# Four tiles of products with the raw x ahead of the first norm, with the norm's factor put in where they are evicted

## The reference

```python
def rms_norm(x, g):
    xf = x.astype(jnp.float32)
    y = xf * lax.rsqrt(jnp.mean(xf * xf, axis=-1, keepdims=True) + EPS)
    return (y * g.astype(jnp.float32)).astype(x.dtype)
...
    h = rms_norm(x, norm_g)
    q, k, v, z = jnp.split(h @ w_in, 4, axis=-1)
    q = rms_norm(q.reshape(b, s, DA_HEADS, 2, DA_HEAD), q_norm_g) * (DA_HEAD ** -0.5)
    k = rms_norm(k.reshape(b, s, DA_HEADS, 2, DA_HEAD), k_norm_g)
    v = v.reshape(b, s, DA_HEADS, DA_VDIM)
```

## Time and profile before

| | |
|---|---|
| median of 3 runs | 1915.85 us |
| profiled execution, its own time | 1915.09 us |
| its span | 1913.3 us |
| TensorE (PE) busy | 1873.1 us, 98% |
| VectorE (DVE) busy | 988.9 us, 52% |
| ScalarE (ACT) busy | 815.8 us, 43% |
| GpSimd (POOL) busy | 124.2 us, 6% |
| DMA | 201.95 MB, mean 106 GB/s |
| mean granted clock of TensorE | 0.994 |

### The profile page before, as it was taken

The page is one execution under the profiler, slowest core; times in us unless marked ns, Lnnn a source line. Parts: engine busy times, 40 slices in busy tenths (PEclk is TensorE's granted clock), DMA queues, the critical chain, the costliest instruction groups (busy, mean ns, idle before and its releaser), DMA issues.

```text
span 1913.3 us, 22366 instructions
## 1 busy us (share of the span) xinstructions
PE 1873.1 (98%) x8923; PEld 1452.5 (76%) x8923; DVE 988.9 (52%) x1764; ACT 815.8 (43%) x1325; POOL 124.2 (6%) x148
## 2 busy tenths in 40 slices
PE   7999999999999999999999999999999999999997
PEld 4666666666788788888886777677888878888886
DVE  4566667666544643333347566854434673333322
ACT  5466556656643342222324555434432342222221
POOL 0111111110001000000010011000000100000000
PEclk9999999999999999999999999999999999999999
DMA  5334334332233132222223222221023322322221
GB/s 213 147 144 150 137 143 155 143 144 99 78 118 123 69 110 99 94 96 92 99 95 117 93 72 88 84 94 34 34 96 113 121 89 99 99 93 97 97 93 62
DMA packets 56526, 201.95 MB, mean 106 GB/s; under 512 B 6478, under 2 KB 6934, under 8 KB 55784
## 3 DMA queue, kind: packets, MB, share of 16 engines
q1 hardware_dynamic: 44616, 158.32, 23.6%
q0 software_dynamic: 11808, 42.21, 6.1%
HBM read 195.23 MB, written 5.28 MB: 105 GB/s over the span
## 4 chain that ended last, share of the span: by engine, by line
PE 76%; DVE 12%; ACT 9%; issue 2%; DMA 1%; POOL 0%; DVEq 0%; SPq 0%; ACTq 0%
PE ps L1111 22%; PE ps L1114 22%; PE ps L1112 22%; ACT wH L1820 2%; DVE wL L1404 2%; PE ps L1209 2%; PE ps L1173 1%; DVE a L1533 1%; PE ps L1197 1%; DVE a L1699 1%; ACT a L1931 1%; PE ps L1185 1%; PE ps L1245 1%; PE ps L1144 1%; DVE b L1464 1%
## 5 line engine op out<-in xcount | busy, mean ns | idle before, releaser
L1111 PE MATMUL ps<-hH,wH 128*128 128x512 f32 x1592 | 649.3, 408 | 7.6 <-ACT wH L1820 5.9
L1114 PE MATMUL ps<-hH,wL 128*128 128x512 f32 x1592 | 623.7, 392 | 0.2 <-DVE wL L1404 0.2
L1112 PE MATMUL ps<-hL,wH 128*128 128x512 f32 x1592 | 622.6, 391 | 0.0
L1404 DVE TENSOR_TENSOR wL<-wr,wH 128x1024 fp32r<-128x1024 f32 (+2 forms) x285 | 345.1, 1212 | 526.7 <-ACT wH L1820 526.5
L1820 ACT ACTIVATE wH<-wr 128x1024 fp32r<-128x1024 f32 (+2 forms) x285 | 295.0, 1036 | 239.8 <-PE ps L1114 226.1
L1111 PEld LDWEIGHTS ps<-hH,wH 128*128 128x128 f32 x1592 | 299.7, 188 | 104.6 <-issue 36.2
L1114 PEld LDWEIGHTS ps<-hH,wL 128*128 128x128 f32 x1592 | 299.0, 188 | 66.2 <-DVE wL L1404 1.1
L1112 PEld LDWEIGHTS ps<-hL,wH 128*128 128x128 f32 x1592 | 300.0, 188 | 62.6 <-issue 6.2
L1111 PE MATMUL ps<-gffn,wH 128*128 128x512 f32 x400 | 157.4, 394 | 1.0 <-DVE xT L1618 1.0
L1112 PE MATMUL ps<-gffn,wH 128*128 128x512 f32 x400 | 156.3, 391 | 0.0
L1114 PE MATMUL ps<-gffn,wL 128*128 128x512 f32 x400 | 156.2, 390 | 0.0
(11 more groups left out here) (301 smaller groups left out, 2049.6 us busy)
## 6 DMA issues: line engine op xcount, KB each, us to landing
wr<-wst SPq DMA_DIRECT2D x268, 512.0 KB, 3.5
a<-wfd POOLq DMA_DIRECT2D x54, 512.0 KB, 4.7
xT<-wfd POOLq DMA_DIRECT2D x18, 512.0 KB, 7.0
wr<-wst SPq DMA_DIRECT2D x16, 384.0 KB, 3.0
xT<-xin SPq DMA_DIRECT2D x8, 256.0 KB, 4.9
xT<-xin SPq DMA_DIRECT2D x2, 1024.0 KB, 6.1
xsave<-xT SPq DMA_DIRECT2D x1, 2048.0 KB, 7.9
c<-wfd POOLq DMA_DIRECT2D x8, 256.0 KB, 3.1
```

Of the source, the lines that this page charges most:

```text
L1111: e.matmul(o, hi, xh[k], start=k == 0, stop=False)
L1112: e.matmul(o, hi, xl[k], start=False, stop=False)
L1114: i = e.matmul(o, lo, xh[k], start=False, stop=k == t.nk - 1)
L1404: e.tensor_tensor(dst, x, hi.bitcast(F32), ALU.subtract).then_inc(s[name], 1)
```

## The change

The mean over x that the norm divides by is one number for each token, a column here. It can be put in behind the product: (x g r) W = ((x g) W) r. The changed kernel makes the first four tiles (q, k and v of head 0, q of head 1) from `r0H`, `r0L`, the split x times the gain, and multiplies by the factor r (now in the buffer `row`) at the eviction, on VectorE. The squares' sums stand among the products. The normed x itself is made afterwards, two chunks at a time, between the evictions and the splits; two buffers hold the scaled chunks where there were four. SyncE loads the first two slots of weights among the chunks of x. silu(c) is made with an exponential and a reciprocal instead of ScalarE's Silu. The small work of head 1's steps 0 to 7 stands in one block behind q of head 1. `two` and `norm` go; the last norm is `out_norm`.

```diff
@@ class Plan @@
-        self.norm(4, "out")
+        self.out_norm()
...
+    def first_tiles(self, tq, tk, tv, tq1):
+
+        free = [("rs", 0)] * 4
+
+        def chunk(c):
+            self.raw(0, c)
+            free[c % 4] = self.square(0, c, v=("first", c % 4), free=free[c % 4])
+
+        def mm(t, *ks):
+            for k in ks:
+                self.add("mm", t=t, k=k)
+
+        tiles = [tq, tk, tv, tq1]
+        for t in tiles:
+            self.slot(t, 0)
+            t.done = t.slots[-1] + 1
+        chunk(0)
+        chunk(1)
+        self.add("split", j=0)
+        mm(tq, 0, 1)
+        chunk(2)
+        chunk(3)
+        self.add("split", j=1)
+        mm(tq, 2, 3)
+        mm(tk, 0, 1, 2, 3)
+        for c in range(4, 8):
+            chunk(c)
+            if c == 7:
+                self.add("split", j=2)
+            mm(tq, c)
+            mm(tk, c)
+        mm(tv, *range(8))
+        rs = self.sig("rs")
+        self.add("norm_rs", n=0, stat=8, rs=rs)
+        self.add("rnd", both=[self.sig("rnd"), self.sig("rnd")])
+        for name in ("nv", "nh", "nl"):
+            self.count[name] = 8
+        self.add("split", j=3)
+        mm(tq1, *range(8))
+
+        def out(t):
+            self.add("out_" + t.kind, t=t, done=t.done, rs=rs, **t.more)
+            self.add("split", j=t.slots[0] + NSPL)
+
+        self.chunks(0, 0, 2, rs)
+        self.add("out_qk", t=tq, done=tq.done, rs=rs, **tq.more)
+        self.chunks(0, 2, 4, rs)
+        yield "q"
+        out(tk)
+        self.chunks(0, 4, 6, rs)
+        yield "k"
+        self.chunks(0, 6, 8, rs)
+        out(tv)
+        yield "q1"
+        out(tq1)
@@ attention, loop over the heads @@
                 if i == 0:
-                    self.two(qk(0, 0), qk(0, 1), lambda: sq_lo(0, "q"))
-                    for step in range(16):
+                    first = [qk(0, 0), qk(0, 1), v(0), qk(1, 0)]
+                    for t in first:
+                        t.rhs = "r"
+                    start = self.first_tiles(*first)
+                    sq_lo(0, next(start))
+                    sq_lo(0, next(start))
+                    next(start)
+                    tiles = []
+                elif i == 1:
+                    while step < 8:
                         run(step)
-                    step = 16
-                    tiles = tiles[2:]
+                        step += 1
+                    first[3].more["d"]["sum_free"] = sq_free[1]
+                    for _ in start:
+                        pass
+                    tiles = tiles[1:]
@@ model_kernel @@
+        G = Arena(P0, "g0", 8192, F32R)
+        r0H, r0L = G.several(8), G.several(8)
...
             if n == 0:
-                return qn[0], [c5(t, j) for t in Wr for j in range(2)]
+                return row, [c5(t, j) for t in Wr for j in range(2)]
...
@@ SyncE @@
             for c in range(8):
                 e.dma_start(c5(xT, c), x_d[:, 512 * c:512 * c + 512]).then_inc(s_x[c], 16)
+                if c in (0, 2):
+                    weights(c // 2)
@@ TensorE @@
                 elif what == "square":
-                    if d["c"] == (0 if d["n"] == 0 else 7):
+                    if d["n"] == 0:
+                        w.wait_ge(s["first"], 16)
+                        w.wait_ge(s["nsq"], d["nsq"])
+                        e.matmul(ps[7][:], C("one1024"), square_view(d), start=d["c"] == 0, stop=d["c"] == 7).then_inc(s["stat"], 1)
@@ VectorE @@
+                elif what == "out_qk":
+                    t, d2 = d["t"], d["d"]
+                    if t.rhs == "r":
+                        w.wait_ge(s["slot"], t.done)
+                        w.wait_ge(s["rs"], d["rs"])
+                        e.tensor_tensor(qk_raw[d2["m"] % 4], ps[t.bank][:], norm_views(0)[0], ALU.mult).then_inc(s["qe"], 1)
...
                     w.wait_ge(s["slot"], t.done)
-                    if d["h"]:
+                    if t.rhs == "r":
+                        e.tensor_tensor(vT0, ps[t.bank][:], norm_views(0)[0], ALU.mult).then_inc(s["ve"], 1)
+                    else:
                         w.wait_ge(s["vt"], d["h"])
-                    e.tensor_copy(vT0, ps[t.bank][:]).then_inc(s["ve"], 1)
+                        e.tensor_copy(vT0, ps[t.bank][:]).then_inc(s["ve"], 1)
@@ ScalarE @@
-                    e.activation(csil, S("c"), ACT.Silu).then_inc(s["csil"], 1)
+                    e.activation(csil, S("c"), ACT.Exp, scale=-1.0)
```

More of the change, by code:

```diff
@@ L181, in whole @@
             if k == 5 and then is not None:
-                then()
-    def two(self, t0, t1, then=None, ahead=False):
-        self.slot(t0, 0)
-        self.slot(t1, 0)
-        for k in range(8):
-            self.add("mm", t=t0, k=k)
-            self.add("mm", t=t1, k=k)
-        for t in (t0, t1):
-            t.done = t.slots[-1] + 1
-            if ahead:
-                self.add("split", j=t.slots[0] + NSPL)
-        for t in (t0, t1):
-            self.add("out_" + t.kind, t=t, done=t.done, **t.more)
-            if not ahead:
-                self.add("split", j=t.slots[0] + NSPL)
-            if t is t0 and then is not None:
                 then()
@@ L271, in attention @@
         add("start")
-        for c in range(8):
-            self.square(0, c)
-        self.norm(0, "plain")
-        add("rnd", both=[sig("rnd"), sig("rnd")])
         st = [{} for _ in range(HEADS)]
-        qk_free, rs_free = [("nl", 8)] * 4, [("nl", 8)] * 4
+        qk_free, rs_free = [("rs", 1)] * 4, [("nl", 8)] * 4
         sq_free = [0, 0]
@@ L280, in attention, with tile @@
         n_qk = [0]
-        def tile(kind, col, **d):
-            return Tile(kind, src("l0_w_in", col), pb.take()[1], "h", None, n=0, **d)
+        def tile(kind, col, bank=None, **d):
+            return Tile(kind, src("l0_w_in", col), pb.take()[1] if bank is None else bank, "h", None, n=0, **d)
         def qk(h, w):
@@ L1421, in _ @@
                     e.tensor_scalar(lam, lam, LAM0, None, ALU.add, ALU.bypass).then_inc(s["lam"], 1)
+                    own(e.tensor_scalar(csil, csil, 1.0, None, ALU.add, ALU.bypass))
+                    own_done()
+                    own(e.reciprocal(csil, csil))
+                    own_done()
+                    e.tensor_tensor(csil, csil, S("c"), ALU.mult).then_inc(s["csil"], 1)
                 elif what == "norm":
-                    n = d["n"]
-                    rs, tmp = norm_views(n)
@@ new lines, in _ @@
+                    for c in range(8):
+                        e.scalar_tensor_tensor(ob[c], X[c], scale_col(4, c), rs_f, ALU.mult, ALU.mult).then_inc(s["ob"], 1)
+                elif what == "out_qk":
[4 more added lines that the diff above has]
+                        e.tensor_tensor(qk_raw[d2["m"] % 4], ps[t.bank][:], norm_views(0)[0], ALU.mult).then_inc(s["qe"], 1)
@@ L1454, in _ @@
                     w.wait_ge(s["rh"], d["rh"])
+                    if n == 0:
+                        w.wait_ge(s["small"], 16)
+                        w.wait_ge(s_x[c], 16)
                     e.scalar_tensor_tensor(xl[c], X[c], scale_col(n, c), xh[c].bitcast(F32),
@@ L1902, in _ @@
                     m = d["m"]
[L1903 to L1905 removed]
+                    if t.rhs == "h":
+                        w.wait_ge(s["slot"], t.done)
+                        w.wait_ge(s[d["free"][0]], d["free"][1])
+                        e.activation(qk_raw[m % 4], ps[t.bank][:], ACT.Copy).then_inc(s["qe"], 1)
                     w.wait_ge(s["qe"], d["qe"])
```

131 lines of the change are left out of this document (48 added, 83 removed).

## The result

The changed kernel takes 1922.34 us (median of 6 runs, 1921.55 to 1924.49), the kernel before, on the same chip, 1915.15 us (6 runs, 1914.05 to 1916.16). The ratio is 1.004 with a 95% interval of 1.0027 to 1.0053: slower, by 7.2 us, where the text above said 8.5 us (1924.4 us). Its profiled execution took 1921.55 us with a span of 1919.7 us.

The account below looks back on a forecast made before the run. TensorE, busy 98%, was taken as the bound, its largest stop 5.9 us. 7.4 + 2.4 - 1.3 = +8.5 us on 1915.09 us gave 1923.6 us, with 0.76 us for the median 1924.4 us; range 1919 to 1928 us.

Parts of the forecast that it names:

- Loads, ScalarE and TensorE up to the factor: Start of the kernel: products from 10.45 us, norm factor near 28.3 us, q of head 1 ending at 39.25 us.
- From the factor to the last normed x: Serial work on VectorE and ScalarE, 19.3 us (14.0 before), puts the last normed x at 47.6 us, not 30.91.
- TensorE behind tile v: TensorE waits 5.2 us for k's squares, then for ada loads; k of head 1 starts near 58.2 us, +7.4 us.
- Two products at half pace end the step (0.85 us): End of first ada step: after the last load lands at 57.3 us, two half-clock products take 0.85 us.
- Clock: TensorE restarts at half clock for 3.8 to 5.9 us after its stops, costing +2.4 us (1.9 to 2.9).
- What comes back: TensorE's earlier 1.28 us wait at 68.84 us for the next head's k squares goes, booked at -1.3 us.
- The lead is kept: Rival: k of head 1 starts at 42.0 us, 8.8 us early, 1905.8 us; last normed x before 39.5; chance 0.04.
- GpSimd is held up: Rival: GpSimd's issue of four ada loads stalls 3.3 us during VectorE's work, giving 1927.7 us; chance 0.10.
- The clock holds: Rival: scattered ada products keep TensorE's clock up, so 2.4 + 0.4 us go, giving 1921.6 us; chance 0.10.

Follow-up runs that it names:

- Experiment 5: Changed kernel with chunks 2 to 7 of the normed x in one piece ahead of q's low half and k's eviction and square: 1917.36 us.
- experiment 4: Changed kernel with 46 unread products in TensorE's two stops (20 before k's sum, 26 before the first ada product): 1924.72 us.
- experiments 7 and 8: Changed kernel with a fifth raw tile: small work of heads 0 to 3 put later, 1929.94 us; other places for work of heads 0 and 1, 1921.99 us.
- experiments 10 and 11: Changed kernel with squares' sums first, three raw tiles, later ada steps, three early ada loads: 1910.03 us; same with ada steps and loads put back: 1918.12 us.

## Why the prediction was right

*Loads, ScalarE and TensorE up to the factor.* x1 was split from 8.00 us, products started at 10.38 us (10.45 booked), the factor came at 28.56 us (28.3) and q of head 1 ended at 39.75 us (39.25). Clock and durations were taken from rows of the same operations, and it shows.

*From the factor to the last normed x.* 28.56 to 48.02 us are 19.5 us, 19.3 booked. This sum, made of VectorE's and ScalarE's order item by item, carried the verdict. Experiment 5 shows that its place is what matters: without one instruction less the kernel gains 5 us.

*TensorE behind tile v.* k's sum at 45.46 us after 5.09 us of standing (44.9 and 5.2 booked); the first load issued at 48.34 us, the last 1.8 us later; landing in 7.7 us (7.6 taken, nearer to the 8.1 than to the 6.2 of the earlier trace rows). The term that was mis-sized is the one behind: "Two products at half pace end the step (0.85 us)". The last load's four records, of two products, took 1.8 us from the start of the first to k of head 1 (57.82 to 59.62 us). The kernel shows why: each load feeds two of the four groups of output rows.

```python
                    for k in d["ks"]:
                        for j in range(n):
                            a = at + j // 2
...
                            i = e.matmul(ps[7][32 * j:32 * j + 1, :], csil[:, k:k + 1],
```

Here n is 4 and `a` numbers the loads. Where all four loads are there, as in the kernel before, all four groups work side by side, and the 16 records of the step run from 48.15 us to the next product in 1.83 us:

```profile
48.15 1.46 PE L1209 MATMUL ps<-a,tiny 128*1 128x512 f32 x10
...
49.98 0.50 PE L1111 MATMUL ps<-hH,wH 128*128 128x512 f32 x1
```

I had priced them as two ordinary products at half clock, 0.43 us each, which is near a quarter of the 1.83 us, doubled. A load by itself fills two groups only: 0.96 us at full clock (experiment 4, 58.78 to 59.74 us), 1.80 us at half. With these 0.95 us, and the last landing 0.5 us later than booked (57.8, not 57.3 us), k of head 1 starts 8.84 us later, not 7.4.

*Clock.* 2.4 us booked, about 0.7 us found behind the step: the clock was up after 1.4 us of products, not after 3.8 to 5.9 us. The stop of the earlier trace rows that I had as a model was followed by products alone; here 7 us of scattered ada products went ahead. That they shortened the return is my reading; no run takes them away alone. Experiment 4 puts the whole of the clock near 1.6 us, with the ada step. The two errors nearly cancel, 8.84 + 0.7 - 1.3 = 8.2 us against the 8.5 us booked, and 8.2 us were measured there: the mechanism is right, but that the sum is this near is luck.

*What comes back.* The 1.28 us of the earlier trace rows are gone, as booked: VectorE's scores are taken up at 62.91 us, as soon as TensorE has made them.

*The rest of the program.* The prediction had nothing there. The span of the profiled executions grew by 6.4 us and not by 8.2. The clock's dip at 655 us, which the execution of before had and that of the changed kernel had not, takes 0.5 us off the lag. Then TensorE waits 2.85 us instead of 1.47 us for a load (c<-wfd, at 1050 and 1043 us), and 0.47 us instead of 1.78 us for ScalarE (at 1223 and 1215 us), which nearly cancel. The last 1.6 us come from a second dip that only the execution of before had: its granted clock is 0.91 from 1300 to 1320 us, against 1.00 in the same stretch of the changed kernel (1308 to 1328 us). So the smaller growth of the span is in the main the luck of two executions; the medians differ by 7.2 us.

*The rivals.* "The lead is kept" failed at the place named: the last normed x was there at 48.0 us, not at 39.5. "GpSimd is held up": the four issues took 1.80 and 0.54 us, as in the earlier trace rows, with VectorE at work through all of them. The Trainium skill (page "SBUF — State Buffer", the box on VectorE blocking DMAs) has GpSimd locked out while VectorE runs an operation in a two-port mode, such as a float32 copy from SBUF to SBUF. The prediction took this for any operation of VectorE; from 48.0 to 51.3 us it ran v's eviction, a low half of weights and two scalings, each with two tensor inputs, so these issues do not test the rule. "The clock holds" did not occur, the clock being at 0.50 up to 60.5 us; but its 1921.6 us lie nearer to the measured 1922.34 us than my 1924.4 us do, since the fall cost much less than booked.

## What to carry to other kernels

Work that fills a stop of the busiest engine is a gain only if what it pushes back is not waited for: follow the displaced chain through the other engines to its last consumer, DMA issues included, before counting the stop as won. When a factor is deferred to the eviction, try the reduction first and only as many deferred tiles as the chain behind it is long, and give the loads that hang on the chain's last buffer a place of their own; here it was these together that made a gain of 5.6 us, and without the places of the loads there was none. In a program ordered by hand, moving small work brought new stops that were dearer than the lead that the move was to use (experiments 7 and 8); which of the distances matter was not separated.

## What the runs showed of the hardware

The ada products have one output row each and go to four different groups of output rows. One load's two products, which fill two of the groups, take 0.96 us at full clock and 1.80 us at half, but the eight products of a step, with all four loads there, take only 1.83 us at full clock. The Trainium skill (page "TensorE: Matmul & The Clock Gate", Part 3) says that small matmuls in different tiles of the array run at the same time; the rows agree: the 16 records one behind the other, at the 0.43 us of a record of the squares' sums, would be 6.9 us.

The clock's fall is not settled by the length of a stop alone: between 650 and 670 us the same instructions with the same stops of up to 1.7 us gave a granted clock of 1.00 over 40 us in one execution and of 0.91 in others. The same stop of 2.27 us, in experiments 10 and 11, ends at full clock in one (the record behind it takes 0.47 us, at 34.79 us) and at half in the other (0.77 us, at 34.58 us). What decides between the two, these runs don't show.
